# Memory keys projected at the start, attention three steps deep, decay sums two levels at a time

## What is computed

```python
# block 1
hx = modulate(rms_norm(x, g_pre_mix), sh_m, sc_m)      # sh, sc, gt from silu(c) @ w_mod
hc = modulate(rms_norm(ctx, g_pre_mix), csh_m, csc_m)
att_x = latent_attention(rope(qa_x), rope(ka_x), va_x, ka_c, va_c)      # 8 heads, 512 keys
ret_x = bidir_retention(rope(qr_x), rope(kr_x), vr_x, lg_f, lg_b, st_f, st_b)   # 8 heads
x = x + gt_m * rms_norm(merge_heads(att_x, ret_x, gr_x, w_out), g_post_mix)
x = x + gt_f * rms_norm(swiglu(modulate(...)), g_post_ffn)
# block 2
x = x + 0.5 * swiglu(rms_norm(x))
...                                                     # hgrn2 recurrence and a convolution
kv = rms_norm(mem, mem_norm) @ w_kv_mem                 # 256 rows of memory: keys, values
x = x + softmax(q_mem @ km.T / 16) @ vm @ w_o_mem
x = x + 0.5 * swiglu(rms_norm(x))
```

## Time and profile before

| | |
|---|---|
| median of 3 runs | 1080.62 us (1078.61 to 1081.18) |
| the profiled execution | 1077.97 us |
| its span | 1076.0 us |
| PE busy | 1029.7 us, 96% |
| DVE busy, ACT busy | 601.8 us, 490.4 us |
| read from memory | 187.00 MB |

### The profile page before, as it was taken

One profiled execution on the slowest core, in us unless ns is written; L12 is line 12 of the kernel. 1 busy time (PEld: TensorE's weight loads), 2 busy tenths in 40 slices (PEclk: granted clock), 3 DMA queues, 4 the chain that ended last, 5 costly groups with the idle time before them and its releaser, 6 DMA issues.

```text
span 1076.0 us, 13375 instructions
## 1 busy us (share of the span) xinstructions
PE 1029.7 (96%) x5212; PEld 838.7 (78%) x5212; DVE 601.8 (56%) x699; ACT 490.4 (46%) x581; POOL 0.2 (0%) x4
## 2 busy tenths in 40 slices
PE   4799999999999999999999999999999999999996
PEld 0577768887788888888888887788987778888885
DVE  1672765576855555475555544865675555555543
ACT  3343445536644444355344434573355445443531
POOL 0000000000000000000000000000000000000000
PEclk9799999999999999999999999999999999999998
DMA  9766573212455545546555555443343236545540
GB/s 371 293 263 246 178 291 118 79 40 97 179 193 192 184 170 196 196 158 234 178 192 175 186 187 215 167 157 118 118 146 128 81 125 224 196 162 192 193 157 39
DMA packets 26543, 188.71 MB, mean 175 GB/s; under 512 B 2945, under 2 KB 3201, under 8 KB 3969
## 3 DMA queue, kind: packets, MB, share of 16 engines
q1 hardware_dynamic: 25920, 185.63, 47.4%
q10 hardware_dynamic: 576, 2.43, 0.6%
HBM read 187.00 MB, written 1.05 MB: 175 GB/s over the span
## 4 chain that ended last, share of the span: by engine, by line
PE 86%; DVE 7%; DMA 3%; ACT 2%; issue 1%; SPq 0%; DVEq 0%; ACTq 0%
PE bank L1683 24%; PE bank L1685 24%; PE bank L1684 24%; DMA raw<-in_weights 3%; DVE w_lo L1072 2%; PE bank L1750 2%; PE bank L1911 1%; PE bank L2020 1%; PE bank L1900 1%; PE bank L1739 1%; ACT w_hi L582 1%; PE bank L2114 1%; PE bank L2224 1%; PE bank L1950 1%; PE bank L2206 1%
## 5 line engine op out<-in xcount | busy, mean ns | idle before, releaser
L1072 DVE TENSOR_TENSOR w_lo<-raw,w_hi 128x2048 fp32r<-128x2048 f32 (+1 forms) x151 | 338.9, 2247 | 272.5 <-ACT w_hi L582 272.4
L582 ACT ACTIVATE w_hi<-raw 128x2048 fp32r<-128x2048 f32 x148 | 283.0, 1916 | 274.5 <-PE bank L1685 241.7
L1683 PE MATMUL bank<-w_hi,hT_hi 128*128 128x512 f32 (+1 forms) x864 | 341.7, 396 | 6.9 <-issue 3.0
L1685 PE MATMUL bank<-w_hi,hT_lo 128*128 128x512 f32 (+1 forms) x864 | 335.6, 388 | 0.0
L1684 PE MATMUL bank<-w_lo,hT_hi 128*128 128x512 f32 (+1 forms) x864 | 335.2, 388 | 0.0
L1683 PEld LDWEIGHTS bank<-w_hi,hT_hi 128*128 128x128 f32 x864 | 162.5, 188 | 48.5 <-issue 10.5
L1685 PEld LDWEIGHTS bank<-w_hi,hT_lo 128*128 128x128 f32 x864 | 162.5, 188 | 34.2
L1684 PEld LDWEIGHTS bank<-w_lo,hT_hi 128*128 128x128 f32 x864 | 162.7, 188 | 31.9 <-issue 0.2
L1683 PE MATMUL bank<-w_hi,gT_hi 128*128 128x512 f32 x264 | 103.3, 391 | 0.0
L1685 PE MATMUL bank<-w_hi,gT_lo 128*128 128x512 f32 x264 | 102.8, 389 | 0.0
L1684 PE MATMUL bank<-w_lo,gT_hi 128*128 128x512 f32 x264 | 102.7, 389 | 0.0
(11 more groups left out here) (263 smaller groups left out, 989.5 us busy)
## 6 DMA issues: line engine op xcount, KB each, us to landing
raw<-in_weights SPq DMA_DIRECT2D x172, 1024.0 KB, 4.8
arena<-in_const ACTq DMA_DIRECT2D x1, 1088.0 KB, 5.2
x_res<-in_x SPq DMA_DIRECT2D x1, 1024.0 KB, 7.9
arena<-in_ctx SPq DMA_DIRECT2D x1, 1024.0 KB, 9.9
memKT<-in_mem SPq DMA_DIRECT2D x1, 1024.0 KB, 10.3
out<-xn SPq DMA_DIRECT2D x2, 512.0 KB, 2.7
arena<-in_const SPq DMA_DIRECT2D x1, 770.0 KB, 6.3
rows<-in_final_norm ACTq DMA_DIRECT2D x1, 512.0 KB, 4.7
```

Source lines behind the costliest of these rows:

```text
L582: act.activation(w_hi[:, v_slot, :], raw[:, u_slot, :], ACT.Copy).then_inc(hi_ready, 1)
L1072: ins = dve.tensor_tensor(w_lo[:, v_slot, n], raw[:, u_slot, n], w_hi[:, v_slot, n].bitcast(F32), ALU.subtract)
L1683: pe.matmul(out, hi, rhi, start=start, stop=False)
L1685: return pe.matmul(out, lo, rhi, start=False, stop=stop)
```

## The change

**Keys first.** The units of the memory's keys become the first four weight units (W_K = 0). The memory is loaded first, into `memV`, normed and transposed before x. `key_products` (the 64 quanta, unchanged) are taken between the eight modulation units. The eight modulation units of the first group have five buffers of their own, and of the sixteen later ones every second one is loaded into `memV`, outside the ring. `kr` is issued in a new way (`first_unit`): both units of x, then both of the context, each as 8 products hi·hi, 8 lo·hi, 8 with the weights' low part.

**Attention** has no quanta of keys. Scores run three steps ahead (`AHEAD`), with a third bank and a third buffer of probabilities, and weighted values follow two steps behind. Only one weight unit (W_OUT + 2) is split inside.

**Retention** has none either. Two sets of `q_dec` and `q_decayed` replace one; the exponents of the two outer blocks of the decay matrix are formed by ACT itself (scale), log 2 on the diagonal's exponent replaces the identity on DVE. `gain_diag` and its inputs are computed in the attention stage instead of in retention.

**Decay sums** take two levels with one weight load: 256 columns, one instruction for two. The copy of `cross` goes from DVE to ACT, and the convolution goes behind the last level's products.

The core of the diff:

```diff
+W_K = 0
+W_IN = W_K + 4
+W_OUT = W_IN + 11
...
-HIGH_STEPS = {0: W_KV + 2, 6: W_KV + 3, 11: W_OUT}
-LOW_STEPS = {1: (W_KV + 2, 0), 2: (W_KV + 2, 1), 7: (W_KV + 3, 0), 8: (W_KV + 3, 1), 12: (W_OUT, 0), 13: (W_OUT, 1)}
-HIGH_HEADS = {2: W_OUT + 1}
-LOW_HEADS = {2: W_OUT + 1}
...
+AHEAD = 3
+HIGH_STEPS = {0: W_OUT + 2}
+LOW_STEPS = {2: (W_OUT + 2, 0), 3: (W_OUT + 2, 1)}
...
+            sp.dma_start(mem_in[:], io["mem"]).then_inc(sem("mem_loaded"), 16)
+            mod_in(0)
+            unit_in(W_K)
+            mod_in(1)
+            unit_in(W_K + 1)
+            mod_in(2)
+            sp.dma_start(x[:], io["x"]).then_inc(sem("x_loaded"), 16)
+            mod_in(3)
+            unit_in(W_K + 2)
+            mod_in(4)
+            mod_in(5)
+            unit_in(W_K + 3)
+            mod_in(6)
+            mod_in(7)
+            unit_in(W_IN)
+            unit_in(W_IN + 1)
+            sp.dma_start(ctx_in, io["ctx"]).then_inc(sem("ctx_loaded"), 16)
+            for q in range(4):
+                filled(sp, ("memT", q))
+            for u in range(W_IN + 2, HEAD_UNITS):
+                unit_in(u)
+                kind, v = STREAM[u]
+                if kind == "w" and v in OWN_MODS:
+                    m = OWN_MODS[v]
+                    if m > MOD_K:
+                        sp.wait_ge(mod_used, m - 1)
+                    sp.dma_start(own_mod, io["own_mods"][(m - MOD_K) // 2]).then_inc(sem("own_mod_loaded"), 16)
...
+            norm_stats(mem_in, lambda e: e.wait_ge(sem("mem_loaded"), 16))
+            norm_scale(mem_in, mem_in)
+            split_to(W_K + 1)
+            split_T("memT", col("mem_norm"), hi=memT_hi)
+            split_to(W_K + 2)
             norm_stats(x, lambda e: e.wait_ge(sem("x_loaded"), 16))
             norm_scale(x, xn)
+            keys_out(0)
+            split_to(W_K + 3)
+            keys_out(1)
+            split_to(W_K + 4)
+            keys_out(2)
+            mod_row_out(0)
+            split_to(W_IN + 1)
+            keys_out(3)
+            split_T(None, shifted=True, hi=hT_hi, qs=[0, 1])
+            split_to(W_IN + 2)
             norm_stats(ctx_in, lambda e: e.wait_ge(sem("ctx_loaded"), 16))
-            norm_scale(ctx_in, rows)
-            split_to(W_IN + 1)
-            mod_row_out(0)
-            for n in range(4):
-                if n in (1, 2):
-                    split_to(W_IN + 1 + n)
-                split_T(None, shifted=True, hi=[hT_hi, hcT_hi][n % 2], qs=[2 * (n // 2), 2 * (n // 2) + 1])
+            norm_scale(ctx_in, ctx_in)
+            split_T(None, shifted=True, hi=hT_hi, qs=[2, 3])
+            split_T(None, shifted=True, hi=hcT_hi, qs=[0, 1])
+            split_to(W_IN + 3)
+            split_T(None, shifted=True, hi=hcT_hi, qs=[2, 3])
...
-                if s >= 2:
-                    filled(act, ("probsT", s - 2))
-                act.activation(probs[:, s % 2, :], bank_of(("scores", s))[:, :], ACT.Exp, scale=HD ** -0.5,
+                if s >= AHEAD:
+                    filled(act, ("probsT", s - AHEAD))
+                act.activation(prob_bufs[s % AHEAD], bank_of(("scores", s))[:, :], ACT.Exp, scale=HD ** -0.5,
...
-                act.activation(decay_mats[r % 2], decay_arg, ACT.Exp).then_inc(sem("decay_mat"), 1)
+                m = decay_mats[r % 2]
+                act.activation(m[:, 0:P], c1("bwd_dist", 0, P), ACT.Exp, scale=lg_rows[:, 8 + r:9 + r])
+                act.activation(m[:, 2 * P:3 * P], c1("fwd_dist", 2 * P, 3 * P), ACT.Exp, scale=lg_rows[:, r:r + 1])
+                act.activation(m[:, P:2 * P], decay_arg, ACT.Exp).then_inc(sem("decay_mat"), 1)
...
-                if r:
-                    act.wait_ge(sem("q_decayed"), r)
+                if r >= 4:
...
-            def level_decays(level):
-                for blk in range(TB):
-                    b = filled(act, ("decay", level, blk))
-                    if blk == 0 and level >= 2:
-
-                        filled(act, ("pairs", level - 2, 1))
-                    act.activation(qk_dec[level % 2][:, blk * 512:(blk + 1) * 512], b[:, :], ACT.Exp)\
-                        .then_inc(read_sem(("decay", level, blk)), 1)
+            def level_decays(p, blk):
+                for hp in range(2):
+                    b = filled(act, ("decay", p, blk, hp))
+                    if blk == 0 and hp == 0 and p >= 2:
+                        filled(act, ("pairs", 2 * p - 3, 1))
+                    at = blk * 512 + hp * 256
+                    act.activation(dec_sets[p % 2][:, :, at:at + 256].rearrange("p l (h t) -> p h l t", t=P),
+                                   b[:, :].rearrange("p (h l t) -> p h l t", l=2, t=P), ACT.Exp)\
+                        .then_inc(read_sem(("decay", p, blk, hp)), 1)
...
+            level_decays(0, 0)
+            split_to(W_IN2 + 8)
+            level_decays(0, 1)
...
-                level_decays(step)
+                if 0 < step < LEVELS:
+                    level_decays((step + 1) // 2, (step - 1) % 2)
...
-                chain(dve.tensor_scalar(decay_arg, c1("fwd_dist"), lg_rows[:, r:r + 1], None, ALU.mult))
-                dve.scalar_tensor_tensor(out=decay_arg, in0=c1("bwd_dist"), scalar=lg_rows[:, 8 + r:9 + r], in1=decay_arg,
+                chain(dve.scalar_tensor_tensor(out=decay_arg, in0=c1("fwd_dist", P, 2 * P), scalar=lg_rows[:, r:r + 1], in1=twice,
+                                               op0=ALU.mult, op1=ALU.add))
+                dve.scalar_tensor_tensor(out=decay_arg, in0=c1("bwd_dist", P, 2 * P), scalar=lg_rows[:, 8 + r:9 + r], in1=decay_arg,
                                          op0=ALU.mult, op1=ALU.add).then_inc(sem("decay_arg"), 1)
...
-                    if r:
-                        dve.wait_ge(sem("ret_step"), r)
+                    if r >= 4:
+                        dve.wait_ge(sem("ret_step"), r - 2)
+                    q_decayed, q_dec = q_decayeds[r // 2 % 2], q_decs[r // 2 % 2]
...
-                chain(dve.tensor_tensor(m[:, P:2 * P], m[:, P:2 * P], ident, ALU.add))
...
+                if g == 0:
+                    pe.wait_ge(sem(f"mod_loaded{m}"), 16)
+                    w = first_mod[m % len(first_mod)]
+                elif m % 2 == 0:
+                    pe.wait_ge(sem("own_mod_loaded"), 16 * ((m - MOD_K) // 2 + 1))
+                    w = own_mod
+                else:
+                    u = RAW_AT[("mod", m)]
+                    pe.wait_ge(raw_ready[u % RING], 16 * (u // RING + 1))
+                    w = raw[:, u % RING, :]
...
+            mod_unit(0)
             pe.wait_ge(sem("fixed_loaded"), 16)
-            pe.wait_ge(sem("xn_a"), 1)
-            pe.wait_ge(sem("xn_v"), 1)
-            first_transposes(FIRST_T[0:2])
+            transpose_input("memT", mem_in)
+            mod_unit(1)
+            for q in range(4):
+                read_out(pe, ("memT", q))
+            take(key_products(0), 16)
+            mod_unit(2)
+            take(key_products(1), 16)
+            pe.wait_ge(sem("xn_a"), 2)
...
+            mod_unit(3)
+            take(key_products(2), 16)
...
+            keys = key_products(3)
+            take(keys, 8)
+            mod_unit(6)
+            take(keys, 4)
+            mod_unit(7)
+            take(keys, 2)
             mod_T(0)
-            first_transposes(FIRST_T[3:4])
...
+            def first_unit(stage, v, half, tiles, outs, after_high=None):
+
+                pe.wait_ge(hi_ready, v + 1)
+                for e in range(4):
+                    if e % 2 == 0:
+                        pe.wait_ge(sem("T_hi"), 4 + FIRST_T.index((stage, 2 * half + e // 2)) + 1)
+                    for (hi, lo, tb), out in zip(tiles, outs):
+                        pe.matmul(out[:, :], hi[:, 4 * half + e, tb * P:(tb + 1) * P], w_hi[:, v % RING, e * 512:(e + 1) * 512],
+                                  start=(half == 0 and e == 0), stop=False)
+                if after_high:
+                    after_high()
+                inputs(stage, half)
+                for e in range(4):
+                    for (hi, lo, tb), out in zip(tiles, outs):
+                        pe.matmul(out[:, :], lo[:, 4 * half + e, tb * P:(tb + 1) * P], w_hi[:, v % RING, e * 512:(e + 1) * 512],
+                                  start=False, stop=False)
+                pe.wait_ge(split_ready, v + 1)
+                for e in range(4):
+                    for (hi, lo, tb), out in zip(tiles, outs):
+                        ins = pe.matmul(out[:, :], hi[:, 4 * half + e, tb * P:(tb + 1) * P],
+                                        w_lo[:, v % RING, e * 512:(e + 1) * 512], start=False, stop=(half == 1 and e == 3))
+                if stage == "ctxT":
+                    ins.then_inc(split_used, 1)
+
+            def context_T():
+                pe.wait_ge(sem("xn_a"), 3)
+                pe.wait_ge(sem("xn_v"), 3)
...
+            first_unit("xT", W_IN, 0, both[:2], outs)
+            context_T()
+            first_unit("xT", W_IN + 1, 1, both[:2], outs)
```

(45 more changed lines are left out.)

280 lines of the change are left out of this document (134 added, 146 removed).

## The result

| | before | after |
|---|---|---|
| median | 1080.01 us (1078.61 to 1081.18, 4 runs) | 1062.14 us (1060.61 to 1063.49, 4 runs) |
| the profiled execution | 1077.97 us | 1061.17 us |
| its span | 1076.0 us | 1059.4 us |
| PE busy | 1029.7 us | 1020.1 us |

The ratio is 0.9835, with a 95% interval of 0.9814 to 0.9855: 17.9 us less. The forecast was 1060.5, its range 1053 to 1069. In the profiled executions the kernel became 16.8 us faster where 20 were forecast. That the median came closer than this is luck of the sample, so the working is held against the profiled executions here.

What follows compares the result with a forecast made beforehand. PE was taken to bound the kernel, with 86% of the chain of waits. Terms -17.5 - 0.5 - 8 - 6 + 12 = -20 took 1077.97 to 1058; with 2.65 for the median, 1060.5 us, range 1053 to 1069.

Steps and rivals of the forecast that it cites:

- Attention: Attention stage: three key quanta leave each of 16 steps, 3.25 us falls to 2.15; 17.5 us saved.
- Rival (a): Attention: the step's round trip bounds instead of PE's work, 2.7 us a step; 9 us come back, 1069; chance 0.12.
- The wait ahead of attention: Before attention: PE's 1.29 us wait for ACT's query copies shrinks; 0.5 us saved, between 0 and 1.3.
- Retention: Retention stage: without keys a head takes 2.46 us; 8 us saved, 5 if DVE's chain bound it.
- Decay sums: Recurrence: 64 matmuls of 256 columns take 8.3 us against 13.9; 6 us saved, between 5.5 and 6.5.
- The start: Start up to `kr`: keys half hidden in transfer waits, `kr` near 55 us; 12 us lost, between 9 and 17.
- (c): Decay sums gain only 3 us, 256-column matmuls starting 0.165 us apart; 1063.5; chance 0.07.
- (b): Weight ring starves early: projections wait two or three times for 3 us, or chain before `kr` takes 8; 1068.5; chance 0.11.
- (d): Start: PE stays at its lower clock, 1.2 GHz, costing 29 us more; 1089, slower than before; chance 0.04.
- (e): Better: waits in retention and attention vanish wholly (10 and 18.5 us), the start costs 9; 1055; chance 0.06.

Runs made afterwards that it cites:

- e4: Changed kernel with attention scores two steps ahead in place of three: step still 2.19 us, attention 39.87 us against 39.13.
- e5: Changed kernel with one set of `q_dec` and `q_decayed` again: retention 24.35 us, 2.9 more than the changed kernel.
- e3: e2 with decay sums of one level (128 columns) per matmul: first sums to output projection 77.81 us, 6.27 more than e2; span 1061.0 us.
- e2: Changed kernel, recurrence's end reordered: DVE keeps last pairs before the convolution, ACT does table, high part before `cross` copy, `zg` before next weight copy: stage 71.54 us, span 1055.5.
- e7: Changed kernel with the copy of `cross` on DVE again: `cross` to output projection 6.58 us against 8.59.
- e6: Changed kernel with DVE's convolution before the products of `cross` again: waits 1.10 us ahead of `cross` and 2.02 ahead of the output projection.

## Why the prediction came out as it did

The mechanism was right: PE's work decides, the keys' quanta leave two stages that PE fills, and are half hidden in a start that waited for transfers. By its steps:

- **Attention.** The step was forecast at 2.15 us and is 2.19. The stage gave 18.8 us and not 17.5. The forecast counted 16 equal steps and left out what stood at the end: in the last three steps before, PE also waited 0.33, 0.32 and 0.69 us for ACT's copy ahead of L1911, and those went with the rest. The argument for it, though, was wrong: it held that three steps in flight were needed to keep a round trip of 6.45 us. That number was an upper bound from a stage that PE bound, and e4 shows 4.4 or less. Rival (a) had lived on the same bound, so its 0.12 was too much.
- **The wait ahead of attention.** All of the 1.29 us went, where 0.5 was taken.
- **Retention.** 8.2 us for 8. A head takes 2.65 us and not 2.46, for the scores take 0.92 with `retained` behind them and not 0.73; the heads have no waits, as hoped. The second set that makes this so was worth 2.9 us by e5. The working gave it no price of its own.
- **Decay sums.** The price was right (6.27 us, e3 against e2), though not by its own sum: 7.7 us and eight changes of 0.13 are 8.7 and not 8.3, which would have left 5.2. A group of eight matmuls of 256 columns takes 0.95 us with its change of operands (745.66 to 746.61 after), so the eight groups take 7.6. And the term was still wrong by 2.85, because it took the sums for the whole edit. "Each of these ends when PE ends", with DVE busy for 47.4 of 77.5 us, "so it has room", was read from busy times over the whole stage. At its last 15 us that isn't so. The copy of `cross` on ACT was costed at nothing, without naming what stands behind it in ACT's queue, and nothing was put down for DVE having less time for the same chain once PE's sums are shorter. That is the step that failed. e7 prices the first at 2.0 us. The second is the wait of 1.09 ahead of `cross`, which is gone in e2, where the last pairs are kept ahead of the convolution. The convolution's new place was costed at nothing too, and rightly (e6).
- **The start.** `kr` came 2.4 us later than forecast. The first key was at 21.23 and not at 20.1 (1.1); the first 22 key matmuls were 0.213 apart in place of 0.12, 2.1 us where 1.3 was allowed (0.8); the returns to the keys, from modulation units and transposes, cost 0.1 to 0.2 each (0.8 in all). Four quanta and not two stand behind the last modulation unit, which gave 0.7 back. The chain from that unit's last matmul to `kr` was 4.0 us (53.41 to 57.41) and not 3.6. Part of this is the one execution: in the eight profiles of this start without an edit to it, the first key stands at 19.8 to 21.4 and `kr` at 55.2 to 58.1. In `kr` there were waits of 0.80 and 0.17 us for the context's norm and its high part, 0.7 more than allowed.

**The rivals.** (c) gave the nearest time to what came, 1063.5 against 1062.1, and for the wrong reason: its matmuls of 0.165 us are 0.12. (b) found nothing: in the projections of block 1 no wait of PE for a weight part is recorded, and the chain ahead of `kr` took 4.0 us and not 8. (d) was right that the clock is at half in the start and wrong on its length: it lasted 4.8 us behind the first key and cost 2.1, not 29. (e) had attention nearly right (18.5) and the start wrong (9 where 13.6 were lost).

## What to carry to other kernels

When a copy is moved to an engine with idle time, read what is queued behind it there: a short instruction that waits for the last product holds up table loads, weight copies and bank releases that could have gone first. Busy shares over a stage tell nothing of its last few microseconds, so follow every engine's queue through the last products to the first one of the next stage. And an upper bound that comes from a stage bound by another engine is no measure of a latency; a cheap test with one step less in flight is.
